# Two-stack model on one core: five gate tiles of the recurrent layer and the attention scores beside them change places

## The reference, cut to what matters

```python
def griffin_swa_mixer(u, w_in, ...):
    proj = u @ w_in
    gate, xr, q, k, v = jnp.split(proj, ...)          # 1024, 1024, 1024, 128, 128 columns
    xr = causal_dwconv(xr, conv_w, conv_b)
    y_a = jax.nn.gelu(gate, approximate=True) * rg_lru(xr, w_a, b_a, w_x, b_x, lam)
    y_b = swa_sink_alibi(q..., k..., v..., sinks)
    return jnp.concatenate([y_a, y_b], axis=-1) @ w_out
```

```python
    s = q @ k.T * scale - slope * distance            # masked outside the window
    mx = max(s.max(-1), sink)
    p = exp(s - mx);  p = p / (p.sum(-1) + exp(sink - mx))
    o = p @ v
```

## Time and profile before

| what | value |
|---|---|
| median of 3 runs | 1397.73 us (1397.54 to 1397.87) |
| the profiled execution's own time | 1397.55 us |
| its span, from the first to the last instruction | 1395.5 us |
| busy share of the span: PE, DVE, ACT, POOL | 98%, 75%, 60%, 39% |
| chain of work that ended last: PE, DVE, ACT | 79%, 11%, 4% |
| mean granted PE clock | 0.998 |
| bytes read from HBM | 231.57 MB, 167 GB/s over the span |

### The profile page before, as it was taken

The page is one execution under the profiler, slowest core; times in us unless marked ns, Lnnn a source line. Parts: engine busy times, 40 slices in busy tenths (PEclk is TensorE's granted clock), DMA queues, the critical chain, the costliest instruction groups (busy, mean ns, idle before and its releaser), DMA issues.

```text
span 1395.5 us, 31671 instructions
## 1 busy us (share of the span) xinstructions
PE 1372.0 (98%) x13503; PEld 1174.4 (84%) x13503; DVE 1052.0 (75%) x1395; ACT 831.9 (60%) x1283; POOL 550.6 (39%) x449
## 2 busy tenths in 40 slices
PE   9999999999999999999999999999999999999997
PEld 7778888888778888888778888889888788888887
DVE  6897885557797884567887898756978765798853
ACT  5684554337675544446895756545776777575652
POOL 0144995122056991225210575603213211366610
PEclk9999999999999999999999999999999999999999
DMA  9543566554343666534336365552643333366551
GB/s 363 184 145 128 172 212 211 189 166 151 123 147 105 234 213 211 185 103 166 126 118 242 123 215 193 182 191 93 218 146 122 107 122 137 137 242 212 191 172 31
DMA packets 37020, 234.66 MB, mean 168 GB/s; under 512 B 4752, under 2 KB 7824, under 8 KB 10384
## 3 DMA queue, kind: packets, MB, share of 16 engines
q1 hardware_dynamic: 36880, 232.63, 48.7%
HBM read 231.57 MB, written 1.05 MB: 167 GB/s over the span
## 4 chain that ended last, share of the span: by engine, by line
PE 79%; DVE 11%; ACT 4%; issue 3%; POOL 1%; DMA 1%; SPq 0%; ACTq 0%; DVEq 0%; POOLq 0%
PE psum L733 22%; PE psum L734 22%; PE psum L735 22%; DVE low L2402 4%; ACT high L1733 2%; PE psum L818 1%; PE psum L819 1%; PE psum L820 1%; DMA raw<-stream 1%; PE psum L943 1%; PE psum L939 1%; POOL h L3215 1%; POOL m L3213 1%; DVE arena L2509 1%; ACT m L2135 0%
## 5 line engine op out<-in xcount | busy, mean ns | idle before, releaser
L2402 DVE SCALAR_TENSOR_TENSOR low<-raw,high 128x2048 f16<-128x2048 f32 (+5 forms) x247 | 532.4, 2162 | 188.2 <-ACT high L1733 187.6
L733 PE MATMUL psum<-u,high 128*128 128x256 f16 (+2 forms) x2008 | 552.7, 275 | 0.4 <-ACT arena L1719 0.3
L735 PE MATMUL psum<-u,low 128*128 128x256 f16 (+2 forms) x2008 | 552.4, 275 | 0.0
L734 PE MATMUL psum<-u,high 128*128 128x256 f16 (+2 forms) x2008 | 552.4, 275 | 0.0
L1733 ACT ACTIVATE high<-raw 128x2048 f16<-128x2048 f32 (+4 forms) x248 | 417.3, 1686 | 121.3 <-PE psum L735 88.6
L733 PE MATMUL psum<-arena,high 128*128 128x256 f16 (+2 forms) x1112 | 304.7, 274 | 1.3 <-DVE arena L2919 1.0
L735 PE MATMUL psum<-arena,low 128*128 128x256 f16 (+2 forms) x1112 | 304.7, 274 | 0.0
L734 PE MATMUL psum<-arena,high 128*128 128x256 f16 (+2 forms) x1112 | 304.7, 274 | 0.0
L733 PEld LDWEIGHTS psum<-u,high 128*128 128x128 f16 x2008 | 196.5, 98 | 33.4 <-issue 4.5
L734 PEld LDWEIGHTS psum<-u,high 128*128 128x128 f16 x2008 | 196.7, 98 | 29.0 <-issue 0.7
L735 PEld LDWEIGHTS psum<-u,low 128*128 128x128 f16 x2008 | 196.6, 98 | 28.1
(11 more groups left out here) (368 smaller groups left out, 1836.5 us busy)
## 6 DMA issues: line engine op xcount, KB each, us to landing
raw<-stream SPq DMA_DIRECT2D x206, 1024.0 KB, 4.8
raw<-stream SPq DMA_DIRECT2D x8, 768.0 KB, 4.2
raw<-stream SPq DMA_DIRECT2D x5, 512.0 KB, 3.6
raw<-stream SPq DMA_DIRECT2D x2, 896.0 KB, 4.5
con<-consts SPq DMA_DIRECT2D x1, 1437.0 KB, 12.2
h<-x_t SPq DMA_DIRECT2D x2, 512.0 KB, 6.0
raw<-stream SPq DMA_DIRECT2D x2, 448.0 KB, 5.5
misc<-small SPq DMA_DIRECT2D x1, 512.0 KB, 13.5
```

The lines of the kernel that those rows point to most:

```text
L733: pe.matmul(out, w_hi, x[0], start=start, stop=False)
L734: pe.matmul(out, w_hi, x[1], start=False, stop=False)
L735: return pe.matmul(out, w_lo, x[0], start=False, stop=stop)
L2402: tell(dve.scalar_tensor_tensor(low[:, at:at + w], raw[:, off:off + w], W_SCALE, high[:, at:at + w], ALU.mult, ALU.subtract), split_ready ...
```

## The change

Nothing is computed otherwise. In PE's list the scores of the units 2 to 6 and the gate tile that followed each of them change places: the tiles 0, 1, 2, 4 and 5 now come first. Tile 3 stays where it was, between scores(4) and values(2), and the lists of the other engines are the same.

```diff
--- before.py
+++ after.py
@@ -1485,25 +1485,25 @@
                     lru_gate(n)
                 one(GQ[7])
                 turn(0)
+                one(GG[0])
                 scores(2)
-                one(GG[0])
                 values(0)
                 turn(1)
+                one(GG[1])
                 scores(3)
-                one(GG[1])
                 values(1)
                 turn(2)
+                one(GG[2])
                 scores(4)
-                one(GG[2])
                 one(GG[3])
                 values(2)
                 turn(3)
+                one(GG[4])
                 scores(5)
-                one(GG[4])
                 values(3)
                 turn(4)
+                one(GG[5])
                 scores(6)
-                one(GG[5])
                 values(4)
                 turn(5)
                 one(GG[6])
```

## The result

The first comparison gave 1402.21 us as the median of 8 executions of the changed kernel (1400.09 to 1403.93), beside 1397.80 for 8 of the kernel before (1397.43 to 1401.55): a ratio of 1.0026 on record, interval 1.0016 to 1.0037 (an estimate that is not quite the quotient of the two medians; the same holds for the ratios below). The forecast was 1398.6, its range 1397.4 to 1399.6. Twice 12 further executions of the same kernel gave 1400.21 and 1399.86, both 1.0014 (1.0002 to 1.0027 and 1.0003 to 1.0024). The change makes the kernel slower, by more than was forecast, and three comparisons of one kernel differ by 2 us. Both have one explanation, which shows in two steps: first the stretch that was changed, then PE's granted clock.

The account below looks back on a forecast made before the run. PE is busy nearly always, but the DVE-ACT chain sets the stretch's end. PE's waits grow from 3.1 to 4.4 us, less 0.09 for each of five turns: 0.9; 1397.73 + 0.9 = 1398.6 us, range 1397.4 to 1399.6.

Parts of the forecast that it names:

- the table above: Seven steps from turn(1) to the output product, timed from turn(0) before, as forecast and after; output product 44.87, 45.77, 45.80 us.
- unit 2's 0.41 given back at turn(1): PE's 0.41 us wait before scores(2) is saved, then lost again at turn(1), which waits for POOL's multiply.
- values(2) 1.0 earlier: At unit 4 PE starts values(2) at 699.43, 1.10 us earlier, with the 0.83 wait before scores(4) won.
- DVE held 0.75 at biased(5): DVE waits about 0.75 us for PE's scores of unit 5, so biased(5) starts 1.01 us late.
- the new wait at values(4): PE waits 1.60 us before values(4) for ACT's copy of unit 4's turned weights, starting 0.33 us late.
- the output product 0.9 later: ACT's last output copy comes at most 0.97 us late; 0.9 taken for it, the output product and all behind.
- a wait of 1.55: PE's wait before the output product, 1.01 us before the change, forecast at 1.55 us after it.
- the absorbed: Rival at biased(5): scores(5) come by 704.39, DVE is not held, only PE's lead grows; about 1397.6 us, chance 0.18.
- the twice held chain: Rival at biased(6): scores(6) also come too late, a second slip like the first; 1399.6 us, chance 0.08.
- One rule weighed: PE's clock stayed at 1.00 across a 1.01 us wait, so a 1.60 us wait costs itself and no more.
- the rival made from that rule: The wait before values(4) drops PE to 1.2 GHz, so 10.4 us of work takes twice as long: 1409 us, chance 0.02.
- the 0.2 by which runs differ: Run-to-run spread of 0.2 us, added to 0.4 either way from four junctions, giving bounds 1398.0 to 1399.2.

Follow-up runs that it names:

- Unit 5 alone: Only the scores of unit 5 moved behind gate tile 4, against the kernel before: 1400.01 us, ratio 1.0013.
- units 2 and 4 alone: Only the scores of units 2 and 4 moved behind gate tiles 0 and 2, against the kernel before: 1398.71 us, ratio 0.9998.
- first of the three jobs: Both kernels run again without an edit: the kernel before 1398.15 us, the changed kernel 1400.21 us, ratio 1.0014.
- third: Job with all five moves, unfilled (1399.86 us) and with 11 matmuls directly behind values(6) (1398.95), and units 2 and 4 likewise (1397.65, 1398.40).

## Why the prediction was right and wrong

**Right: the stretch.** Each step of the table above came within 0.1 us: unit 2's 0.41 given back at turn(1), values(2) 1.0 earlier, DVE held 0.75 at biased(5), the new wait at values(4) (1.60 forecast, 1.56 found), the output product 0.9 later (0.93) behind a wait of 1.55 (1.53). Unit 5 alone (1.93 lost) and units 2 and 4 alone (0.14 won) confirm that the loss arises at biased(5). The rivals of the absorbed and of the twice held chain are out: DVE did wait for unit 5's scores, and not for unit 6's. In undisturbed executions the change costs 0.96 (first of the three jobs), 1.27 (third, from 1397.61 to 1398.88): 1398.80 and 1398.88 us against the forecast 1398.6.

**Wrong: "One rule weighed", where the prediction says that by the row a wait of 1.60 "costs itself and no more".** The row had a wait of 1.01 with the clock at 1.00 behind it, and it was stretched to one half as long again. Of the rival made from that rule, the kind was right, but place, price and chance were wrong: it set the fall behind values(4) at 10.4 us and gave it 0.02. The fall comes at the output product, whose wait the prediction itself had at 1.55, lasts 3.42 us, costs 1.7 and comes in about three executions of ten (those at 0.997 lie 1.2 to 2.2 us above the undisturbed ones of the same run). Its mean share is (0.31 - 0.04) x 1.7 = 0.5 us. By the Trainium skill, "TensorE: Matmul & The Clock Gate", section "HAM oscillation — how this bites in real kernels", PE's waits can bring the array back to half rate for the work behind them; the waits of its case are of some 3 to 5 us. Here the traces agree in kind, with 0.50 behind a wait of 1.53 in two profiles of seven and none where it was filled, but not in size: in some executions the shorter wait was enough.

**Wrong too: "the 0.2 by which runs differ".** It came from three executions, 1397.54 to 1397.87. Over 103 executions beside the experiments the kernel before goes from 1396.88 to 1405.82. 24 of them are at 0.996 or less; the long fall near 375 us, which two of the profiles above show, cost 3.95 in that of after and 3.48 in that of before (turn(0) at 682.15 in place of 678.67). That is what made the first comparison so large: of its 8 executions of the changed kernel 5 are at 0.996 or less and 3 at 0.997, none undisturbed. At a rate of one in four, five or more of eight come up in some 3 draws of 100 (an estimate). So this was bad luck by all that the later jobs show, and why just that comparison had so many stays open; their equal rates give no sign that the change brings the long fall about. Of 32 executions in all the changed kernel's mean is 1400.86, before's (of 103) 1398.80, 2.1 more. 1.0 of it is the schedule, 0.5 the clock at the output product, and 0.4 the long fall, which the changed kernel drew in 11 of 32 against 24 of 103 (0.11 x 4); together 1.9.

**Open.** Why the wait at values(4), as long as the other, isn't followed by a fall; filling it changed nothing that shows. What decides in which executions a fall comes, and what brings on the falls in the second layer. Whether units 2 and 4 alone are worth having: they win 0.14 in the stretch, and no version here can be told from the kernel before by more than its interval on the faster side.

## What to carry to other kernels

Moving a job of 2.9 us ahead of scores pays only until the next engine in the chain waits for them: compare PE's gain with the time for which the result used to lie ready, unit by unit. A wait that grows is priced with the clock behind it, for each wait that grows and not only for the longest, and matmuls placed directly behind the last work before it test that. Before a difference of 0.2% is forecast, learn the kernel's own spread, compare the executions whose mean granted clock is the same, and look up in the profile where the clock fell: the mean doesn't tell.

## What the runs showed of the hardware

- The granted clock fell to 0.50 without a wait of PE just before, near 375 us, in four profiles of fourteen. By the view by stretches it stayed there for 10.2 us in three of them and 13.7 in one, while PE was busy throughout. Small matmuls of 64x64 with 15 and 30 columns stand ahead of it; as the same ones in the first layer, near 70 us, have no fall behind them in any profile, they alone don't explain it. A mean of 0.996 or less, as these falls leave, came in 55 of 238 executions.
- Behind a wait of 1.53 us it fell for 3.42 us in both profiles that caught it, beginning soon after the output product's first matmul (from the first row of each below 1.00, at about 725.1 behind 724.46 and at 723.4 behind 723.15). Half a microsecond of idle time more, 1.53 for 1.01, took the executions at a mean of 0.997 from 5 of 115 to 24 of 78.
- Matmuls whose results nobody reads, put into that wait, held the clock up: 0 of 45 executions at 0.997. They cost nothing in the stretch where they ended before the wait did (45.79 us beside 45.80), and 0.56 where they started late.
